# Carried products moved between the row tiles of the next projection, and transposes moved around the last outputs, in the state-space rounds of a hybrid encoder block

## The reference

```python
xbc = silu(depthwise_conv_centred(xbc, conv_w, conv_b))     # x, B, C
acs = cumsum(dt * A)                                        # within a chunk
seg = acs[t] - acs[s];  Lm = exp(where(mask, seg, -inf))
CB = einsum('bctgn,bcsgn->bctsg', Cc, Bc)
y_diag = einsum('bctsg,bctsgh,bcsghp->bctghp', CB, Lm, xdt)
states = einsum('bcsgn,bcsgh,bcsghp->bcghpn', Bc, decay_to_end, xdt)
h = dec * h + st                                            # carried from chunk to chunk
y_off = einsum('bctgn,bcghpn,bctgh->bctghp', Cc, prev, exp(acs))
y = (y_diag + y_off) + d_skip * xs;  y = y * silu(z)
```

## Time and profile before

| | |
|---|---|
| median of 3 runs | 2359.41 us |
| the profiled execution, its own time | 2358.79 us |
| span of its instructions | 2357.3 us |
| TensorE busy | 2257.4 us, 96% |
| VectorE busy | 1468.6 us, 62% |
| ScalarE busy | 970.3 us, 41% |
| GpSimd busy | 436.3 us, 19% |
| TensorE's mean granted clock | 0.990 |

### The profile page before, as it was taken

How to read it: one execution, slowest core, us unless ns; L and a number is a source line. 1 busy time by engine, 2 the same in 40 slices (tenths; PEclk the granted TensorE clock), 3 DMA queues, 4 the chain that set the end, 5 groups by cost and what they waited for, 6 DMA issues and landing times.

```text
span 2357.3 us, 36237 instructions
## 1 busy us (share of the span) xinstructions
PE 2257.4 (96%) x13147; PEld 2008.1 (85%) x13147; DVE 1468.6 (62%) x2344; ACT 970.3 (41%) x1467; POOL 436.3 (19%) x304
## 2 busy tenths in 40 slices
PE   6999999998999999999999999999999999999997
PEld 6899999997877677888888888888888899899996
DVE  7667676678788888632544454443136677677677
ACT  6333243344432533432566666553224333243343
POOL 2100000000123433323333333332323100000000
PEclk9999999998999999999999999999999999999999
DMA  3221221213111111123111111111332222231211
GB/s 115 66 73 54 71 72 53 71 53 109 46 37 27 36 36 36 48 80 96 46 46 45 44 39 41 36 40 50 95 129 60 65 77 67 58 85 53 71 54 72
DMA packets 252272, 144.64 MB, mean 61 GB/s; under 512 B 5712, under 2 KB 248576, under 8 KB 252176
## 3 DMA queue, kind: packets, MB, share of 16 engines
q1 hardware_dynamic: 249072, 130.63, 19.9%
q0 software_dynamic: 2336, 12.58, 1.5%
q10 hardware_dynamic: 768, 0.13, 0.0%
HBM read 133.89 MB, written 9.44 MB: 61 GB/s over the span
## 4 chain that ended last, share of the span: by engine, by line
PE 76%; DVE 10%; issue 7%; ACT 5%; POOL 1%; DMA 0%; ACTq 0%; DVEq 0%; POOLq 0%
PE slot L512 29%; PE aux L543 23%; PE slot L592 14%; DVE ca L1882 2%; PE aux L905 1%; PE aux L796 1%; POOL wlo L2234 1%; PE aux L783 1%; PE aux L873 1%; PE aux L898 1%; PE aux L886 1%; DVE e L1963 1%; PE slot L673 1%; PE aux L766 1%; ACT whi L977 1%
## 5 line engine op out<-in xcount | busy, mean ns | idle before, releaser
L2234 POOL TENSOR_TENSOR wlo<-raw,whi 128x1024 fp32r<-128x1024 f32 (+1 forms) x100 | 226.7, 2267 | 1058.4 <-ACT whi L977 1058.4
L512 PE MATMUL slot<-xh,whi 128*128 128x256 f32 (+1 forms) x1360 | 360.6, 347 | 4.9 <-POOL wlo L2234 2.8
L512 PE MATMUL slot<-xh,wlo 128*128 128x256 f32 (+1 forms) x1360 | 351.1, 340 | 0.0
L512 PE MATMUL slot<-xl,whi 128*128 128x256 f32 (+1 forms) x1360 | 349.9, 339 | 0.0
L512 PEld LDWEIGHTS slot<-xh,whi 128*128 128x128 f32 x1360 | 252.2, 188 | 42.5 <-issue 7.0
L512 PEld LDWEIGHTS slot<-xh,wlo 128*128 128x128 f32 x1360 | 255.5, 188 | 30.0
L512 PEld LDWEIGHTS slot<-xl,whi 128*128 128x128 f32 x1360 | 255.5, 188 | 29.8
L543 PE MATMUL aux<-th,whi 128*128 128x392 f32 (+1 forms) x640 | 220.6, 345 | 9.5 <-ACT work L1081 5.6
L1055 ACT ACTIVATE whi<-work 128x512 fp32r<-128x512 f32 x220 | 135.6, 625 | 199.0 <-DVE work L1602 105.1
L543 PE MATMUL aux<-tl,whi 128*128 128x392 f32 (+1 forms) x640 | 216.5, 338 | 0.0
L543 PE MATMUL aux<-th,wlo 128*128 128x392 f32 (+1 forms) x640 | 215.8, 337 | 0.0
(11 more groups left out here) (333 smaller groups left out, 4384.7 us busy)
## 6 DMA issues: line engine op xcount, KB each, us to landing
raw<-in_w_in SPq DMA_DIRECT2D x81, 512.0 KB, 3.9
raw<-in_ffn_w_gate_up SPq DMA_DIRECT2D x48, 512.0 KB, 4.3
work<-in_ffn_w_gate_up SPq DMA_DIRECT2D x40, 512.0 KB, 4.7
raw<-in_ffn_w_down SPq DMA_DIRECT2D x80, 256.0 KB, 3.0
raw<-in_ssd_w_proj SPq DMA_DIRECT2D x8, 512.0 KB, 3.9
raw<-in_hg_w_proj SPq DMA_DIRECT2D x8, 512.0 KB, 4.0
raw<-in_w_out SPq DMA_DIRECT2D x8, 512.0 KB, 3.8
h_spill<-h POOLq DMA_DIRECT2D x1, 3072.0 KB, 11.0
```

The source lines that it names most:

```text
L512: mm = pe.matmul(slot[b][:, PC + u:PC + v], w[b][:, t, :], x[:, t, u + off:v + off], start=(t == 0 and p == 0 and q == 0), stop=(t == k - ...
L2234: pool.tensor_tensor(wlo[s % 2][:, 0:k, :], raw[s % 2][:, 0:k, :], whi[s % 2][:, 0:k, :].bitcast(F32), ALU.subtract).then_inc(w_lo, 1)
```

## The change

Only TensorE's order is changed; no instruction is added or taken away, and the lists of the other engines stay as they are.

- `job` takes a dict `between`; ahead of row tile t it issues what stands there.
- `ssd_carried` issues CB and the carried products of chunks 0 and 1 only. Those of chunks 2, 3, 4 and 5 are issued ahead of row tiles 1, 2, 3 and 4 of the projection that follows (`rest`), each with its wait on `off_ok`. This is done after all four groups.
- `ssd_turn` is cut into three: sets 0 to 3, then chunk 4 of step 4, sets 4 and 5, chunk 5 of step 4, sets 6 and 7. This is done in each of the three rounds; the first group's `ssd_turn` stays whole.

```diff
+                        if t in between:
+                            between[t]()
@@ ssd_carried
-                for c in range(NC):
+                carried_chunks(G, 0, 2)
+
+            def carried_chunks(G, first, last):
+
+                for c in range(first, last):
                     if c >= 2:
                         wait(pe, off_ok, NC, c - 1, G)
@@ ssd_step
                 for c in outs:
+                    if c in between:
+                        between[c]()
                     wait(pe, wy_ok, 2 * NC, 2 * c + 2, G)
...
+            def rest(G):
+
+                return {c - 1: lambda c=c: carried_chunks(G, c, c + 1) for c in range(2, NC)}
@@ first group, and the loop
-            ssd_job(0, (1, None))
+            ssd_job(0, (1, None), rest(first))
...
-                ssd_turn(N)
-                ssd_step(4, G)
+                ssd_turn(N, 0, 4)
+                ssd_step(4, G, {5: lambda: ssd_turn(N, 4, 6)})
+                ssd_turn(N, 6, NC + 2)
...
-                ssd_job(0, (2, g))
+                ssd_job(0, (2, g), rest(N))
```

## The result

| | before | after |
|---|---|---|
| median | 2359.74 us, 6 runs (2357.83 to 2361.35) | 2376.3 us, 6 runs (2372.68 to 2380.58) |
| profiled execution, its span | 2358.79, 2357.3 us | 2373.8, 2372.3 us |
| CB products of the rounds start at | 658.1, 748.3, 840.3, 932.3 us | 657.6, 751.6, 846.7, 942.8 us |
| last output (its transpose, L793 and L802) starts at | 998.0 us | 1013.2 us |
| TensorE's mean granted clock | 0.990 | 0.985 |

The changed kernel is slower: 1.0071 times the time before, 95% interval 1.0058 to 1.0084. That is 16.6 us by the medians and 15.0 us by the two profiled executions. The CB marks say where. From mark to mark, the three rounds take 94.0, 95.1 and 96.1 us instead of 90.2, 92.0 and 92.0, and the stretch from the last CB to the last output 70.3 instead of 65.7 us. From the last output to the end of the span it is 1359.2 us, and it was 1359.3.

What follows compares the result with a forecast made beforehand. TensorE leads the whole chain (76%), but VectorE sets the pace of steps 1 to 3, with 0.43 us of slack. Part A 13.1 + GpSimd 1.6 - part B 2.2 = +12.5 us, median 2371.9 us; range 2361 to 2378 us.

Steps and rivals of the forecast that it cites:

- VectorE's lateness: VectorE leaves the carried products later in four places, and steps 1 to 3 do not make it up: 13.1 us.
- the clock: TensorE's granted clock after new waits ahead of projection 1: -2.6 to +4 us in all, taken as 0.
- part B: Transposes split around the last outputs of step 4: 0.7 us saved in each of three rounds, -2.2 us.
- The slack of 0.43 us and the feeding of VectorE: Carried products: one chunk every 2.13 us, VectorE leaves 3.7 us later in round 1; 0.43 us slack before convolution used up.
- The third segment product: In step 0 it waits about 2 us for VectorE's masks of CB, ending at 768.1 instead of 764.4.
- The 3.3 us that follow: Round 1: the convolution starts 3.3 us later, and this counts in step 1, where TensorE waits for rh.
- part A: Carried products of chunks 2 to 5 ahead of row tiles 1 to 4, in four places: 13.1 us lost.
- GpSimd: rl falls on low of projection 1: nothing to 1.2 us a place, 0.4 taken, +1.6 us for four.
- The rival that interleaving pays: TensorE regains its waits on VectorE in three rounds and part B's 2.2 us: 2350 us; chance 0.12.

Runs made afterwards that it cites:

- one break: Part A with chunks 2 to 5 in one piece ahead of row tile 1, transposes as in the kernel before: 2363.84 us, ratio 1.0016.
- a_only: Part A alone: the changed kernel with the transposes back in one piece: 2371.86 us, ratio 1.0050 to the kernel before.
- ab_again: The changed kernel itself, both parts, run again on another chip: 2378.93 us, ratio 1.0079 to the kernel before.
- a_only_again: The same kernel as a_only, run on another chip: 2373.32 us, ratio 1.0058 to the kernel before.
- a_fill: Part A alone plus extra passes, adding no result, in TensorE's waits of step 0: 2373.49 us, ratio 1.0061 to the kernel before.
- a_fill_again: The filled kernel a_fill, run beside a_only_again on one chip: 2371.28 us, ratio 1.0050 to the kernel before.
- a_wide: Part A alone with the chunks ahead of row tiles 1, 3, 5 and 7: 2400.92 us, ratio 1.0176 to the kernel before.
- best_fill3: One break ahead of row tile 2, earlier low of projection 0, part B, later xdt and rl, fillers ahead of step 3: 2358.58 us, ratio 0.9992.
- b_xdt_later: Part B alone, GpSimd starting step 0's xdt only after VectorE reads the first carried chunk: 2361.42 us, ratio 1.0007 to the kernel before.

## Why the prediction was right, and where not

Forecast +12.5 us on the profiled execution and 2371.9 us; it was +15.0 us and 2376.3. The direction and the range held, and so did the main mechanism, that VectorE's lateness is paid. Its size, the clock and part B did not. Step by step:

**The slack of 0.43 us and the feeding of VectorE: right, slightly over.** A chunk every 2.13 us was forecast, it was 1.94. The 0.19 us of a return stand in place of a pass's 0.22 us, not beside it: the row tile behind chunk 5 starts 0.24 us after the first of its two passes, so the last pass costs nothing more, and I had added both. VectorE left the carried products 3.15 us later in round 1, not 3.7, while over four places its waits grew by 14.5 us, 3.6 us each.

**The third segment product: right.** "Waiting about 2 us" was 2.38 us, 9.3 us in the four places.

**The 3.3 us that follow: too much, by what VectorE won back.** With the clock kept at 1.00 part A costs 1.7 to 2.2 us a place. In round 1 the convolution takes 1.42 + 4.55 = 5.97 us. Before it took 6.86, with rl beside it: 0.99 and

```profile
767.44 5.87 DVE L1882 SCALAR_TENSOR_TENSOR ca<-ci,gw,ca 128x802 f32<-128x802 f32 x4
```

So the lateness shrinks by 0.9 us behind the place for which it was reckoned. The path through step 1 was wrong as well. TensorE was to wait there for rh, and it doesn't: its waits of 0.42 us are gone in after and in the filled kernels, because projection 1, held by `low`, is the later of the two. Ahead of step 2 VectorE leads again, by the same 1.4 us as before.

**GpSimd: wrong place, wrong sign.** +0.4 us a place was taken for `low` of projection 1. That `low` took 1.23 us, as alone, though the third rl started beside it; two of the three rl fell on the masks of CB instead (769.81, 1.95 us), and these took no longer than in the earlier trace rows. GpSimd of after:

```profile
769.23 2.44 POOL L2318 TENSOR_TENSOR rl<-incl,gal 128x512 fp32r<-128x512 f32 x2 [25.82 <-PE aux L790]
...
772.77 1.48 POOL L2318 TENSOR_TENSOR rl<-incl,gal 128x512 fp32r<-128x512 f32 x1 [1.10 <-PE aux L790]
```

The Trainium skill ("SBUF — State Buffer", Who interferes with whom) exempts a VectorE instruction with at most one input in SBUF, outside the two-port modes, and the masks, which no row had shown beside GpSimd, agree with it: 1.95 us beside rl, 1.95 before. The cost that did come was not in the sum: xdt on the first update of the states, 1.36 us in after, in part B.

**The clock: the mis-sized term.** It was put at 0 with +4 us as its worst. Projection 1 took 9.7 to 11.5 us in the four places of after, instead of 8.6, some 7 us in all, and the filled version shows what the places are without it: 1.4 to 2.7 us less each. The waits ahead of step 0's third segment product and of projection 1 were in the prediction, with their place and length; only their weight was judged by one row of step 3.

**The rival that interleaving pays: fallen.** Part A alone costs 0.5 to 0.6%, with one break 0.16%. The rule of the Trainium skill ("Perfetto Trace Analysis", Optimization Strategy) that had spoken for it is not borne out in this stretch.

**Part B: the term that failed.** It was to give 0.7 us a round, three times. TensorE gained 0.98 us a round, more than forecast, and none of it was kept. I had stopped at "TensorE sets the pace from here to the updates" and not asked what comes behind the updates: VectorE, by 2.16 us. Even without the 0.94 us beside xdt the gain would first have become TensorE's waiting. In after it made the wait ahead of row tile 0 2.43 us, 1.50 in a_only. Behind 2.4 us projection 0 ran slow at 3 of the 6 ends of rounds in after and ab_again: the last chunk's products ended 14.3 to 14.4 us after the CB products instead of 12.8. Behind 1.50 us it did so at none of the 12 of a_only, a_only_again, a_fill and a_fill_again (11.9 us). The changed kernel's ratio of 1.0071 and 1.0079 on two chips stands against 1.0050 and 1.0058 for part A alone, about 5 us; the intervals overlap in part and the two were not run side by side, so this is likely and not shown.

In hindsight part A's 12.9 us (profiled execution of a_only) are about 8 of lateness and, as the remainder, 5 of clock, and part B adds some 2 on top (15.0). The forecast had 14.7 for part A's lateness and GpSimd together, 0 for the clock and -2.2 for part B. So lateness and GpSimd were over by nearly 7, the clock was under by 5 and part B by 4. That the sum came within 2.5 us of the measured 15.0 is partly luck.

**Left open.** From the last output to the end, where no kernel here changes anything, the 14 profiled executions took 1358.2 to 1366.9 us. That doesn't go with a shorter state-space part: a_wide, with the longest, took 1365.7 us, and best_fill3, with the shortest, 1366.9. It goes with the granted clock: in windows of 100 us it was 1.00 in all but one (0.98) for before, after and a_only, and 0.97 to 0.99 in three or four for b_xdt_later, a_fill_again, a_wide and best_fill3. These are the windows from 200 to 500 us behind the last output, of before and of best_fill3:

```profile
1198.00:1498.00 300.00, 290.65 (x1905) 255.55 (x1904) 141.41 (x310) 166.01 (x196) 94.80 (x41) 1.00 0.16 41
```
```profile
1191.80:1491.80 300.00, 290.67 (x1839) 255.82 (x1838) 139.89 (x303) 163.60 (x193) 94.77 (x41) 0.97 0.16 41
```

TensorE is as busy and gets 66 matmuls fewer done. Why the clock is lowered there in one execution and not in another stays open, and so does whether a kernel's state-space part has a hand in it.

## What to carry to other kernels

Before moving work of one engine between pieces of another job, read the slack of the engine that consumes it: with 0.43 us of slack, a piece every 1.9 us in place of one every 0.9 us is a loss, whatever the producer's waits seem to promise. Follow a gain past the next handover, up to the engine that ends the wait there, and list which GpSimd instructions slide over which two-input VectorE instructions. When a rearrangement leaves TensorE's waits longer, price what runs behind them at the lower clock as well. And count a gain that shows in one part of one execution only when the medians show it too.

## What the hardware showed unexpectedly

- The same wait is followed by a lowered clock or not: 3.1 us of waiting, thrice in one execution, and the same carried products behind it took 5.9, 5.2 and 3.5 us. Behind 2.4 us ahead of step 3 the passes took 3.4 us in 14 rounds and 4.5 to 4.9 us in 25. With waits of 2.16 us the carried products took 3.54 us in all rounds of before, and 5.20 us in one of b_xdt_later.
- Passes whose result is thrown away, put in TensorE's waits, kept what follows at full speed each time: projection 1 in 8 places of 8 (9.7 to 11.5 us in 16 of 16 without them), step 3 in 3 of 3 (14 of 39 without them). The medians moved by 2 us at most.
- GpSimd beside VectorE: the first update of 0.42 us took 1.36 us beside xdt, three copies of 12 columns 1.54 instead of 0.31 us and `low` 1.91 instead of 1.23 us beside rl, while the masks with an input in PSUM stayed at 1.95 us beside rl.
- State-space parts shorter by 4 to 6 us (last output at 993.6 and 991.8 instead of 998.0) left the medians within 0.1% of before. From one execution to another the unchanged stretch behind them varied by more, 8.7 us, with the granted clock.
